# Three pairs of dilated query and key chunks as token-major seven-product pairs in a two-block fused kernel

## The reference, cut to what matters

```python
def mixer_layer(x, ...):                    # h is x after an rmsnorm
    # one projection h @ w_in, cut by columns into 26 chunks of 512:
    #  0-1 dq, 2-3 dk, 4-5 dv, 6-7 dg     differential attention, 8 heads, two maps of 64
    #  8-10 lq, 11-13 lk, 14-16 lv, 17 lg  dilated attention, 3 groups of 4 heads of 128
    #  18 mq, 19 mg  memory attention, 4 heads of 128;  20-25 three merge gates
    o_a = diff_attention(dq, dk, dv, lam, rel_bias)     # two softmax maps per head, p0 - lam * p1
    y_a = (rmsnorm(o_a) * silu(dg)) @ w_br_diff
    # dilated: scores of lq and lk for each group and head, softmax over the groups
    y_b = (o_b * silu(lg)) @ w_br_dil
    y_m = (memory_attention(mq, mem) * silu(mg)) @ w_br_mem
    merged = gate0 * y_a + gate1 * y_b + gate2 * y_m
    return x + merged @ w_out
```

## Time and profile before

| | |
|---|---|
| time, median of 3 runs | 2062.06 us |
| profiled execution: time, span | 2062.14 us, 2060.4 us |
| TensorE, VectorE, ScalarE, GpSimd busy | 88%, 40%, 19%, 6% |
| granted clock of TensorE, mean over the span | 0.954 |
| DMA over the span | 593.84 MB, mean 288 GB/s |

### The profile page before, as it was taken

The page is one execution under the profiler, slowest core; times in us unless marked ns, Lnnn a source line. Parts: engine busy times, 40 slices in busy tenths (PEclk is TensorE's granted clock), DMA queues, the critical chain, the costliest instruction groups (busy, mean ns, idle before and its releaser), DMA issues.

```text
span 2060.4 us, 34718 instructions
## 1 busy us (share of the span) xinstructions
PE 1803.1 (88%) x14736; PEld 1152.4 (56%) x14736; DVE 819.2 (40%) x1340; ACT 389.0 (19%) x892; POOL 133.5 (6%) x188
## 2 busy tenths in 40 slices
PE   8998776677699877766869999999999999999998
PEld 5665555555557655554554448746554458746553
DVE  6541111111144111111115753473657753473656
ACT  4521011011112100100112122222221122222221
POOL 3100000000000000000001401100221001100000
PEclk9999898899899998889889999999999999999999
DMA  9799999999999999999998674443546374443331
GB/s 353 217 379 420 420 420 421 420 420 420 420 392 388 419 420 421 420 420 420 420 420 318 163 244 156 135 163 123 173 154 213 100 246 154 135 163 123 133 123 62
DMA packets 182598, 593.84 MB, mean 288 GB/s; under 512 B 51236, under 2 KB 52644, under 8 KB 133544
## 3 DMA queue, kind: packets, MB, share of 16 engines
q1 hardware_dynamic: 173896, 572.70, 71.3%
q0 software_dynamic: 8544, 18.89, 3.7%
HBM read 578.95 MB, written 8.39 MB: 285 GB/s over the span
## 4 chain that ended last, share of the span: by engine, by line
PE 57%; DMA 28%; DVE 7%; SPq 5%; issue 2%; ACT 1%; DVEq 0%; ACTq 0%
DMA ring<-in_moe_w_dram 28%; PE ps L651 20%; PE ps L618 9%; PE ps L1686 5%; PE ps L624 3%; SPq L1397 2%; PE ps L1721 2%; PE ps L1668 2%; PE ps L595 1%; PE ps L533 1%; PE ps L1963 1%; PE ps L628 1%; SPq L506 1%; SPq L1406 1%; PE ps L1741 1%
## 5 line engine op out<-in xcount | busy, mean ns | idle before, releaser
L1686 PE MATMUL ps<-ring,xT 128*32 128x128 f32 x8192 | 303.2, 306 | 178.0 <-DMA ring<-in_moe_w_dram 170.9
L1686 PEld LDWEIGHTS ps<-ring,xT 128*32 128x32 f32 x8192 | 262.5, 121 | 244.4 <-DMA ring<-in_moe_w_dram 185.3
L2383 DVE TENSOR_TENSOR arena<-arena,ps 128x256 f32<-128x256 f32 x32 | 13.5, 421 | 561.5 <-ACT arena L2057 561.5
L618 PE MATMUL ps<-xT,ring 128*128 128x256 f32 x896 | 199.2, 380 | 0.9 <-DMA ring<-in_w_in_dram 0.9
L651 PE MATMUL ps<-ring,xT 128*128 128x512 f32 x432 | 194.2, 594 | 0.5 <-ACT xT L785 0.5
L1092 DVE TENSOR_TENSOR ring<-ring 128x2048 f32<-128x2048 f32 x80 | 183.4, 2292 | 20.0 <-PE ps L651 5.9
L618 PEld LDWEIGHTS ps<-xT,ring 128*128 128x128 f32 x896 | 168.0, 190 | 26.7 <-issue 3.3
L1721 PE MATMUL ps<-arena 128*32 128x512 f32 x768 | 120.0, 606 | 31.6 <-DVE arena L2383 31.6
L1330 POOL DMA_DIRECT2D ring<-gap_bias x160 | 96.1, 643 | 786.7 <-DMA ring<-in_w_in_dram 475.5
L1668 PE MATMUL ps<-arena,x_tm 128*128 128x128 f32 x1024 | 137.6, 291 | 0.9 <-issue 0.9
L1668 PEld LDWEIGHTS ps<-arena,x_tm 128*128 128x128 f32 x1024 | 129.1, 205 | 11.6 <-issue 11.6
(11 more groups left out here) (315 smaller groups left out, 2027.4 us busy)
## 6 DMA issues: line engine op xcount, KB each, us to landing
ring<-in_moe_w_dram SPq DMA_DIRECT2D x287, 1024.0 KB, 26.1
ring<-in_w_in_dram SPq DMA_DIRECT2D x52, 2048.0 KB, 9.3
arena<-in_moe_w_dram SPq DMA_DIRECT2D x89, 1024.0 KB, 26.7
ring<-in_w_br_diff_dram SPq DMA_DIRECT2D x4, 2048.0 KB, 10.5
ring<-in_w_out_dram SPq DMA_DIRECT2D x4, 2048.0 KB, 7.9
arena<-in_moe_w_dram SPq DMA_DIRECT2D x14, 512.0 KB, 14.7
ring<-in_w_mem_kv_dram SPq DMA_DIRECT2D x3, 2048.0 KB, 16.3
ring<-in_mla_w_o_dram SPq DMA_DIRECT2D x1, 4096.0 KB, 25.0
```

The costliest lines, as they stand in the source:

```text
L618: m = nc.tensor.matmul(bank[:, u * T:(u + 1) * T], w[:, k, f * P:(f + 1) * P], xT[:, k, :], start=(k == 0), stop=(k == KD - 1))
L1686: m = nc.tensor.matmul(ps[SL * q:SL * q + SL, g % 2, s * P:(s + 1) * P], xs[:, g % 2, k, s * SL:(s + 1) * SL], w[:, c0:c0 + 2 * P - 1:2], ...
```

## The change

Chunks 8/9, 10/11 and 12/13 become pairs. Each is computed token-major into `lin_token`, and VectorE turns each half of 128 tokens in blocks of 32x32 into `lin_blocks` (`turn_linear`), one of them within the pair behind the additions of its second output and one at its end. Sixteen DMAs for each pair (`move_linear`, each of 32 partitions and 16 x 32 words in a partition) carry the blocks into `lqk`; they are issued on SyncE behind the chunk five places after the pair's first, that is behind 13, 15 and 17. Differential heads 0 and 1, 2 and 3, 4 and 5 are now jobs 0 and 1 of these pairs.

The moves of queries and keys become 16 DMAs each, of both token halves at once, and are issued behind chunks 7 and 9 instead of 5 and 7. The buffers `lin_token` and `lin_blocks` lie where `lv` and `lgt` come later, so waits are added: VectorE before the first turn of pairs 10 and 12 for the moves of the pair before; ScalarE before its copy of unit 1 in pairs 10, 12 and 14 for the pair before to be turned, and before its copy of unit 3 in pair 14 for the moves of pair 12; TensorE before the first dilated scores for the last moves. ScalarE squares the output of a job 1 when it is a differential head. The ScalarE copies of chunks 8 to 13 into `lqk` go.

```diff
--- before.py
+++ after.py
@@ -92,11 +92,13 @@
 
 PLAN = layer_plan()
 PAIRS = [i for i, (c, _, _) in enumerate(PLAN)
-         if c == ("br_diff", 0) or (c[0] == "w_in" and c[1] in (0, 2, 4, 6, 14, 16, 20, 22, 24))]
+         if c == ("br_diff", 0) or (c[0] == "w_in" and c[1] in (0, 2, 4, 6, 8, 10, 12, 14, 16, 20, 22, 24))]
 HALVES = [4 if c[0] in ("br_dil", "br_mem") or i in PAIRS else 3 if i - 1 in PAIRS else 2
           for i, (c, _, _) in enumerate(PLAN)]
 LASTS = len(PLAN) - 2
 QUERIES, KEYS = 0, 2
+LINEAR = (8, 10, 12)
+MOVED = [QUERIES, KEYS, *LINEAR]
 ORDER = [(QUERIES, 0), (QUERIES, 2), (KEYS, 0), (KEYS, 2)]
 ORDER += [(i + u // 4, u % 4) for i in (QUERIES, KEYS) for u in (1, 3, 4, 5, 6)]
 ORDER += [(i, half) for i in range(4, LASTS) for half in range(HALVES[i])]
@@ -113,10 +115,12 @@
           ("turned", 0, 0), ("turned", 0, 1), (KEYS, 2), (KEYS, 3), ("turned", 2, 0), ("turned", 2, 1)]
 for _i in PAIRS[2:]:
     COMBOS += (["diff x"] if _i == DIFF_PAIR else []) + [(_i, j) for j in range(4)]
+    if _i in LINEAR:
+        COMBOS += [("turned", _i, t) for t in range(TT)]
 OUT_COMBOS = ["first w", "second w", "s1", "s2", "s4", "fourth w", "third w", "s3"]
 COMBOS += OUT_COMBOS
 MAPS = dict(diff=2, mem=1)
-MOVES = TT * 2 * 2 * 4
+MOVES = 2 * 2 * 4
 TURNS = dict(diff=1, dil=2, mem=1)
 JOB_SCALE = dict(diff=DQ ** -0.5, dil=HD ** -0.5, mem=HD ** -0.5)
 TILES = dict(diff=KD, dil=LH, mem=MH, merged=KD)
@@ -323,7 +327,8 @@
         merged = dgt
         h_tm, x_sq, g_x = places(arena, 12288, AW - 3072, (TT, D), (2 * TT, CW), (D,))
         by_token = {c: carve(arena, 8192 + 2048 * c, TT, D) for c in (0, 2)}
-        by_blocks = {c: carve(arena, 10240 + 2048 * c, TT, D) for c in (0, 2)}
+        lin_token, lin_blocks = places(arena, 2 * KD * T + 2 * TT * D + 2 * LG * LH * T, AW, (TT, D), (LH * 2, TT, HD))
+        by_blocks = {c: carve(arena, 10240 + 2048 * c, D // DQ, TT, DQ) for c in (0, 2)}
         obT, omT, mergedT = places(arena, 8192, 8192 + 6144, (LH, T), (MH, T), (KD, T))
         gate_of = dict(diff=dgt, dil=lgt, mem=mgt)
         turned_of = dict(diff=oaT, dil=obT, mem=omT, merged=mergedT)
@@ -450,6 +455,8 @@
             name, c = PLAN[i][0]
             if name == "w_in" and c < 4:
                 return [by_token[c][:, t, cc * CW:(cc + 1) * CW] for t in range(TT) for cc in range(2)]
+            if name == "w_in" and i in LINEAR:
+                return [lin_token[:, t, cc * CW:(cc + 1) * CW] for t in range(TT) for cc in range(2)]
             if c == 4:
                 return [dv[:, t, cc * CW:(cc + 1) * CW] for t in range(TT) for cc in range(2)]
             if is_diff(i):
@@ -486,25 +493,40 @@
                         sp.wait_ge(sem("up"), uses * NE + last + 1)
                     dst = cslots_wide[s] if chunk[0] in ("br_dil", "br_mem") else cslots[s]
                     sp.dma_start(dst, chunk_source(l, chunk)).then_inc(sem(f"chunk_in{s}"), 16)
-                    if chunk == ("w_in", 5):
-                        move_heads(sp, l, 0)
                     if chunk == ("w_in", 7):
-                        move_heads(sp, l, 2)
+                        move_heads(sp, l, QUERIES)
+                    if chunk == ("w_in", 9):
+                        move_heads(sp, l, KEYS)
+                    if i - 5 in LINEAR:
+                        move_linear(sp, l, i - 5)
 
         def move_heads(sp, l, c):
 
             sp.wait_ge(sem("combined"), combined_for(l, ("turned", c, 1)))
             n = DQ // 2
-            for t in range(TT):
-                for u in range(2):
-                    for m in range(2):
-                        rows = slice(DQ * m + n * u, DQ * m + n * u + n)
-                        for b in range(4):
-                            src = by_blocks[c][n * b:n * b + n, t, m * CW:(m + 1) * CW]
-                            src = src.rearrange("p (h u i) -> p h u i", u=2, i=n)[:, :, u, :]
-                            t0 = t * P + n * b
-                            sp.dma_start(dqk[rows, c // 2 * KD:(c // 2 + 1) * KD, t0:t0 + n], src).then_inc(
-                                sem("heads_in"), 16)
+            for u in range(2):
+                for m in range(2):
+                    rows = slice(DQ * m + n * u, DQ * m + n * u + n)
+                    to = dqk[rows, c // 2 * KD:(c // 2 + 1) * KD, :].rearrange("p h (t x) -> p (h t) x", t=TT)
+                    for b in range(4):
+                        src = by_blocks[c][n * b:n * b + n, KD * m:KD * m + KD, :, n * u:n * u + n]
+                        sp.dma_start(to[:, :, n * b:n * b + n], src.rearrange("p h t i -> p (h t) i")).then_inc(
+                            sem("heads_in"), 16)
+
+        def move_linear(sp, l, c):
+
+            sp.wait_ge(sem("combined"), combined_for(l, ("turned", c, 1)))
+            n, f = DQ // 2, (c - LINEAR[0]) * 4
+            for u in range(P // n):
+                to = lqk[n * u:n * u + n, f:f + KD, :].rearrange("p h (t x) -> p (h t) x", t=TT)
+                for b in range(4):
+                    src = lin_blocks[n * b:n * b + n, :, :, n * u:n * u + n]
+                    sp.dma_start(to[:, :, n * b:n * b + n], src.rearrange("p h t i -> p (h t) i")).then_inc(
+                        sem("heads_in"), 16)
+
+        def wait_moved(eng, l, c):
+
+            eng.wait_ge(sem("heads_in"), (l * len(MOVED) + MOVED.index(c) + 1) * MOVES * 16)
 
         def chunk_loads(s, end=len(PLAN)):
 
@@ -541,8 +563,10 @@
 
             def scores(l, kind, h, J):
                 if h == 0 and kind == "diff":
-                    pe.wait_ge(sem("heads_in"), (l + 1) * 2 * MOVES * 16)
+                    wait_moved(pe, l, KEYS)
                 elif h == 0:
+                    if kind == "dil":
+                        wait_moved(pe, l, LINEAR[-1])
                     wait_taken(pe, l, dict(dil=chunk_of("w_in", 17), mem=chunk_of("w_in", 18))[kind])
                     if kind == "mem":
                         pe.wait_ge(sem("mkv_in"), l * 32 + 32)
@@ -763,7 +787,7 @@
                 assert turned[0] == 2 + (l + 1) * NTURN - (0 if l + 1 < DEPTH else 2) and job_n == NJOB
 
         def by_feature(name, c):
-            return name == "w_in" and (8 <= c < 14 or c == 18)
+            return name == "w_in" and c == 18
 
         def squares(act, l, t):
             for n, c in enumerate((1, 0) if l == DEPTH and t else (0, 1)):
@@ -818,10 +842,7 @@
                 bank = ps[:, bank_at(l, n), :]
                 two = bank.rearrange("p (a b) -> p a b", a=2)
                 taken = taken_of(l, n)
-                if 8 <= c < 14:
-                    f = 4 * (c - 8) + 2 * half
-                    nc.scalar.copy(lqk[:, f:f + 2, :], two).then_inc(taken, 1)
-                elif c == 18:
+                if c == 18:
                     nc.scalar.copy(mqT[:, 2 * half:2 * half + 2, :], two).then_inc(taken, 1)
                 else:
                     nc.scalar.activation(mgt[:, half, :], bank, ACT.Tanh, scale=0.5).then_inc(sem("tanh_ready"), 1)
@@ -848,6 +869,8 @@
                 copy_product(l, i, 0, first_parts[i])
                 if c == 24:
                     wait_taken(act, l, chunk_of("br_dil", 0))
+                if i - 2 in LINEAR:
+                    act.wait_ge(sem("combined"), combined_for(l, ("turned", i - 2, 1)))
                 copy_product(l, i, 1, o12)
                 if job0:
                     act.wait_ge(sem("o_full2"), l * NJOB + job_n + 1)
@@ -858,6 +881,8 @@
                     take_after(after0)
                 if job1:
                     exps(l, *job1, job_n + 1)
+                if i - 2 == LINEAR[-1]:
+                    wait_moved(act, l, LINEAR[-1])
                 copy_product(l, i, 3, o22)
                 if job0 == ("diff", DH - 1):
                     act_root2(act, 3 * l + 3, slice(0, 16))
@@ -865,6 +890,8 @@
                 if job1:
                     act.wait_ge(sem("o_full2"), l * NJOB + job_n + 2)
                     take_turned([PT3[:, m, :] for m in range(TURNS[job1[0]])])
+                if job1 and job1[0] == "diff":
+                    square_head(l, job1[1], job_n + 1)
                 if after1:
                     take_after(after1)
                 pair_tanh(l, i, 1, 1)
@@ -1145,6 +1172,8 @@
                     add_product(i, 4, first_part)
                     add_to(o12, first_part)
                     output_done(i, 1)
+                    if i in LINEAR:
+                        turn_linear(i, 0)
                     if job1:
                         gated(*job1, job_n + 1)
                     gate_pair(i, c, 1, 1)
@@ -1156,6 +1185,8 @@
                     wait_product_taken(v, l, unit_at(i, 5))
                     add_to(o21, first_part)
                     output_done(i, 2)
+                    if i in LINEAR:
+                        turn_linear(i, 1)
                     gate_pair(i, c, 2, 3)
                     gate_pair(i, c, 3, 2)
                     return job_n + (1 if job0 else 0) + (1 if job1 else 0)
@@ -1260,10 +1291,18 @@
```

(10 more changed lines are left out.)

## The result

The changed kernel takes 2103.74 us (median of 4 runs, 2102.91 to 2106.55), before 2062.03: ratio 1.0199 (1.0186 to 1.0212), 41.7 us slower. 2095 was predicted, 2077 to 2107 as the range.

A forecast was written before the change was run, and what follows sets the result against it. VectorE's fixed order in the new two-head pairs was taken as the bound. To 2062.1 us came +22.4 us (new pairs, pair 14, pair 6, moves) and +10.5 us of clock loss, giving 2095 us, range 2077 to 2107.

The forecast's parts named there:

- VectorE's walk: VectorE's fixed order in a two-head pair, from T0 (its opening scores): second turn at 28.4 us, pair 36.7 us.
- The rival with VectorE off the path: Second head's weights in each pair hidden, VectorE not the bound: 27.6 us gained, 2034.5 us; chance 6%.
- The clock: In the new pairs TensorE's clock falls behind the 5.5 us wait: 2.1 us in five of six, +10.5 us.
- The rival of a steady clock: TensorE's clock stays at 2.4 GHz through the waits, all else as forecast: 2084.5 us; chance 22%.
- the 2.1 us waits I take as harmless: TensorE's waits of 2.1 us at the first turns were counted without any clock loss.
- The moves in pair 14: ScalarE's copy of unit 3 waits for pair 12's moves; 0.5 us allowed, +1.0 for both layers (0 to +16).
- signs of being wrong: Second turn finds its weights ready, or a `heads_in` wait holds TensorE, VectorE or ScalarE over 1 us.
- The issue time: Each 64 KB move on SP was taken to issue in the 611 ns of a 32 KB one.
- rival 2: Moves take 1.2 us each, so ScalarE's copy in pair 14 holds TensorE 8 us more a layer: 2111 us; 7%.
- Pair 6: In layer 0 its second unit no longer waits for chunk 7, since the moves stand behind that chunk: -1.8 us.
- The transposes: Rival: VectorE's transposes with strided output cost twice as much, +1.25 us at each of six tails: 2102 us; 5%.

The follow-up runs named there:

- e2: The changed kernel with each weight combination of the three new pairs cut to 512 of its 2048 words: 2064.08 us, ratio 1.0008 to the kernel before.
- e4: The changed kernel with VectorE doing the second head's weights before the first head's gating in the three new pairs: 2088.46 us, ratio 1.0125 to the kernel before.
- e3: The changed kernel with six idle products on TensorE before the second head's turn in the three new pairs: 2089.37 us, ratio 1.0128 to the kernel before.
- e6: The changed kernel's work in another order on TensorE, VectorE and ScalarE, pair 12's moves before chunk 16: 2068.26 us, ratio 1.0026 to the kernel before.
- e7: As e6, with VectorE's fourth combination before the second head's scaling, and that head's turn behind unit 6: 2059.93 us, ratio 0.9987 to the kernel before.
- e5: The changed kernel with pair 12's moves issued before chunks 16 and 17: 2099.69 us, ratio 1.0175 to the kernel before.
- e1: The kernel before with only the queries' and keys' moves changed, 16 each behind chunks 7 and 9: 2061.05 us, ratio 0.9993.
- e9: As e8, with the fourth weight combination of the three new pairs done by GpSimd: 2049.35 us, ratio 0.9936 to the kernel before.
- e8: As e7, with ScalarE copying unit 0 before the first head's exponentials in the new pairs and pair 14: 2060.18 us, ratio 0.9987 to the kernel before.

## Why the prediction was right, and where it was off

**VectorE's walk.** Right, and the whole loss hangs on it. First turn at T0 + 10.1 in all six pairs, as predicted; second turn 28.4 predicted, 28.4 to 28.9 measured. The 0.2 us on average, +1.5 in all, are small: in pair 8 of layer 0 VectorE stood 0.57 us ahead of the addition and not 0.22, and the second head's scale and maxima took 3.33 us (1240.98 to 1244.31) and not 3.2. e2 and e4 confirm it from two sides: shorten the combinations and the loss goes, take 1.5 us out ahead of the weights and 1.6 us leave the way to the second turn (9.6 in six pairs). The rival with VectorE off the path fell.

**The clock.** Right in kind: the wait of 5.5 us brings the 1.2 GHz level, as behind the waits of the expert part. Off in size: it came in six pairs of six and cost 2.4 us each, I took 2.1 in five. e3 measures it by itself: 14.4 us in the six pairs. The rival of a steady clock (2084.5) fell with the profile after. The step "the 2.1 us waits I take as harmless" failed: behind pair 14's 2.05 us wait in layer 1 the unit took 5.37 us, e6 shows the same behind 2.18 us three times in five, and e7 behind 2.10. The waits of 1.84 to 1.92 us at the first turns stayed without a fall in the changed kernel, but in e4 and in e5 one of eight had it (5.29 and 5.30 us for the unit; in e4 0.74 over the next 6.5 us).

**The moves in pair 14.** The mis-sized term: +0.5 a layer was written, 1.2 and 2.1 us of wait were measured, and 1.8 of clock in layer 1. One of the signs of being wrong that the prediction named did come: a wait for `heads_in` of more than 1 us on ScalarE. The copy there waited 6.8 us in layer 0 and 7.7 in layer 1. The sum itself had unit 3 ready at T0 + 18.4 and the moves landed at 20.7, a wait of 2.3 us, so that sign did not fit the sum. The issue time was right, 0.67 us each with the weights out of the way (e5) and not 1.2, so rival 2 is not borne out. By the Trainium skill ("DMA: Bandwidth & Descriptors", the table under Specifications) transfers under 512 B fall short of line rate. In e5 that did not bind: its moves came at their issue time, with a DMA share of 0.51 over them. Wrong was the start: I took 18.8 us to the last issue from the keys' moves, which were ready as soon as the chunks were issued. Pair 12's moves must first wait for the last transpose, at T0 + 4, and from the chunks' issue to the last move it was 21.0 us (1340.11 to 1361.09) and 21.9 in layer 1. e5 puts them ahead of the weights, and the term goes.

**Pair 6.** Right: -1.9 for -1.8, and e1 shows it without the rest.

**The transposes** with their strided output take 1.25 us as before; that rival is out.

The kernel's run-up to the second block, +1.7 in the balance, was in no term and is not the change's: the scores of head 0 start between 1220.7 and 1222.7 us in the profiles of the changed kernel and of e2 to e9, whose work up to there is the same.

What the prediction had not asked is whether the order could be mended. e6 to e9 say yes, but with all four combinations on VectorE a pair gains only 0.5 us, for VectorE itself needs 32.3 us where two single chunks need 32.8, and pair 14 behind them is 3 us longer than before, which nearly eats what pair 8 gains (31.7 and 31.3 us for 34.9 in e7).

## What to carry to other kernels

A scheme that saves an eighth of TensorE's work pays only where the engine that prepares its operands has room: walk that engine's fixed order through the new stage before counting the saving. A wait on the path costs its length and what the clock loses behind it. And a step freed on one engine (e8) is worth nothing until the next engine's own total (here 32.3 us of VectorE) is lowered too, as e9 did by giving one operation to an engine with room.

## What was not expected of the hardware

- In dense work the granted clock fell behind short waits too, at 1.7 to 1.8 us each, and not behind every one of the same length. Counted over the profiles: behind 1.84 to 1.92 us at a first turn in 2 of 40 (after, e2 to e5), behind 2.05 to 2.18 in 5 of 7 (after, e6, e7), behind 3.7 to 4.1 in 5 of 6 (e4, e5), behind 5.3 to 5.6 in 11 of 11 (after, e5). What decides between them was not tried.
- GpSimd's 128x2048 subtraction (4.54 us) did not slow the VectorE operations beside it in e9, each at 0.69 us. In the kernel before, two additions beside a GpSimd multiplication took 3.57 us instead of 1.53, one of them 2.16 instead of 0.69. The rows differ in their operands: these additions read both inputs from SBUF (`arena`), while the operations beside GpSimd in e9 read PSUM (`ps`) or have one input. Whether that is the cause was not tried.

```profile
1376.89 4.21 POOL L1367 TENSOR_TENSOR arena<-arena,tiny 128x1024 f32<-128x1024 f32 x2 [79.32 <-DVEq L1062]
```

```profile
1378.07 3.57 DVE L1102 TENSOR_TENSOR arena<-arena 128x512 f32<-128x512 f32 x2
```
